# A decoder layer in four token chunks instead of three, with 311 instead of 226 expert pairs placed beside them

## The reference

```python
h = rms_norm(x); q, k, v, u, g_att, g_s5 = split(h @ w_in)
att = diff_attention(q, k, v)              # 8 heads, causal; sampled tokens also read 1024 cached rows
s5y = s5_scan(u)                           # diagonal state space model along the tokens
z = gelu(s5y); s5o = z * sigmoid(z @ w_glu + b_glu)
x = x + (sigmoid(g_att) * (att @ w_proj_att) + sigmoid(g_s5) * (s5o @ w_proj_s5)) @ w_out
h = rms_norm(x)
# PEER: per token 8 heads, each picks 16 of 16384 experts
s1, s2 = (h @ w_query) . sub_keys          # two score rows of 128 per head
eidx, gate = top 16 of the sums of the two top-16 lists, softmax
act = gelu(einsum('thkd,td->thk', expert_u[eidx], h))
x = x + einsum('thk,thkd->td', gate * act, expert_v[eidx])
y = rms_norm(x)
```

## Time and profile before

| | |
|---|---|
| median of the runs | 5216.02 us (2 runs, 5215.28 to 5216.76) |
| the profiled execution | 5215.25 us, its span 5213.5 us, 1.8 us around it |
| VectorE busy | 3092.5 us (59%) |
| TensorE busy | 3691.3 us (71%), mean granted clock 0.852 |
| DMA | 1417.77 MB, 272 GB/s over the span |
| first chunk, second, third, tail | 439, 881, 1562, 1582 us |

### The profile page before, as it was taken

How to read it: one execution, slowest core, us unless ns; L and a number is a source line. 1 busy time by engine, 2 the same in 40 slices (tenths; PEclk the granted TensorE clock), 3 DMA queues, 4 the chain that set the end, 5 groups by cost and what they waited for, 6 DMA issues and landing times. The chain is left out here.

```text
span 5213.5 us, 44142 instructions
## 1 busy us (share of the span) xinstructions
PE 3691.3 (71%) x13504; PEld 2091.9 (40%) x13504; DVE 3092.5 (59%) x6901; ACT 1517.0 (29%) x3777; POOL 1331.2 (26%) x1167
## 2 busy tenths in 40 slices
PE   6964888787766757876755454758777777777776
PEld 4542566564343434434444444424222222222221
DVE  4144211316678756768886555658666666666664
ACT  3111011303244321424432222322333333333333
POOL 0000000002312222322222222224444444444443
PEclk9955569898878878988877777879999999999999
DMA  2013123357855768885578788769999999999997
GB/s 78 34 19 1 3 77 130 108 176 301 347 201 206 303 258 344 330 318 199 201 265 305 304 304 311 285 240 363 420 419 417 415 415 410 414 414 406 408 406 324
DMA packets 282269, 1417.77 MB, mean 272 GB/s; under 512 B 44194, under 2 KB 86658, under 8 KB 144546
## 3 DMA queue, kind: packets, MB, share of 16 engines
q0 software_dynamic: 159344, 1129.94, 54.7%
q1 hardware_dynamic: 122306, 284.90, 16.4%
q10 hardware_dynamic: 384, 0.13, 0.0%
HBM read 1371.57 MB, written 40.93 MB: 271 GB/s over the span
## 5 line engine op out<-in xcount | busy, mean ns | idle before, releaser
L807 POOL DMA_INDIRECT arena<-in_uv,arena x1056 | 1262.8, 1196 | 2652.4 <-DVE arena L918 1730.9
L908 DVE CUSTOM_DVE_ANT_0 arena<-arena 128x1024 f32<-128x1024 f32 x1056 | 1288.5, 1221 | 507.2 <-DMA arena<-in_uv,arena 479.4
L1024 PE MATMUL ps<-arena 128*128 128x512 f32 (+1 forms) x2416 | 1148.5, 621 | 428.9 <-ACT arena L993 428.9
L1091 PE MATMUL ps<-arena 128*128 128x256 f32 (+2 forms) x3456 | 1125.2, 487 | 210.3 <-DMA arena<-in_keys 52.2
L1091 PEld LDWEIGHTS ps<-arena 128*128 128x128 f32 x3456 | 693.8, 204 | 606.5 <-issue 384.8
L1024 PEld LDWEIGHTS ps<-arena 128*128 128x128 f32 (+1 forms) x2416 | 439.0, 191 | 1137.8 <-ACT arena L993 664.1
L918 DVE SCALAR_TENSOR_TENSOR arena<-arena 128x1024 f32<-128x1024 f32 x452 | 577.9, 1279 | 157.7 <-ACT arena L983 157.7
L974 ACT ACTIVATE arena<-arena 128x2 f32<-128x2 f32 x528 | 107.0, 203 | 1689.5 <-DVE arena L908 1689.0
L1683 PE MATMUL ps<-ident,arena 128*128 128x128 f32 x512 | 91.1, 339 | 269.3 <-DMA arena<-in_cache_k 243.8
L983 ACT ACTIVATE arena<-arena 128x1 f32<-128x1 f32 x1056 | 253.3, 287 | 17.9 <-ACT arena L974 0.7
L813 POOL DMA_DIRECT2D arena<-in_iota x1 | 0.7, 715 | 936.7 <-POOLq L1962 936.7
(11 more groups left out here) (249 smaller groups left out, 3762.0 us busy)
## 6 DMA issues: line engine op xcount, KB each, us to landing
arena<-in_w_stat SPq DMA_DIRECT2D x216, 512.0 KB, 6.6
arena<-in_cache_k SPq DMA_DIRECT2D x64, 512.0 KB, 6.6
arena<-in_cache_v SPq DMA_DIRECT2D x64, 512.0 KB, 10.9
arena<-in_w_mov SPq DMA_DIRECT2D x14, 2048.0 KB, 12.7
arena<-in_uv,arena POOLq DMA_INDIRECT x1056, 13.0
arena<-in_x SPq DMA_DIRECT2D x16, 512.0 KB, 4.7
arena<-scr_s POOLq DMA_DIRECT2D x64, 128.0 KB, 12.9
scr_s<-arena SPq DMA_DIRECT2D x16, 384.0 KB, 12.0
```

The costliest lines, as they stand in the source:

```text
L807: pool.indirect_dma_start(ring[s % RING], None, dr["uv"], bass.IndirectOffsetOnAxis(ap=idx[:, g % 4, j:j + 1], axis=0)).then_inc(row_in[s ...
L908: nc.vector.tensor_tensor_reduce(ring[s % RING][:, 0:D], ring[s % RING][:, 0:D], h2r[:, b % 2, :], 1.0, 0.0, ALU.mult, ALU.add, act_in[:, ...
L1024: last = nc.tensor.matmul(ps[0:m, 4 * (b % 2) + c, :], diag[:, n % 4, 0:m], ring[s % RING][:, D + 512 * c:D + 512 * (c + 1)], start=start, ...
L1091: last = nc.tensor.matmul(ps[:, bank, 0:w], wbuf[m % NWB][:, kc * P:(kc + 1) * P], moving[:, kc, :], start=(kc == 0), stop=(kc == KC - 1))
```

## The change

The chunks become four: blocks 0 and 1, 2 and 3, 4 and 5, 6 to 8, which are 256, 256, 256 and 288 columns. Each of the later three has a row of its own in the plan: 82, 88 and 141 pairs, 311 in all, so that 217 stay for the tail. With `PAIRS_FRONT` at 311, the v half of 85 more pairs is added by VectorE instead of TensorE. The three rules for when GpSimd loads score rows, h rows and x rows are rewritten for four chunks.

```diff
-        CHUNKS = ((0, 2), (2, 5), (5, NB))
+        CHUNKS = ((0, 2), (2, 4), (4, 6), (6, NB))
         STAGES = ("glu", "s5", "v", "att", "dec", "ga", "out", "query")
         PAIR_PLAN = ((0, 0, 0, 0, 0, 0, 0, 0),
-                     (6, 12, 7, 24, 0, 12, 5, 16),
-                     (7, 14, 9, 27, 50, 14, 6, 17))
+                     (6, 12, 8, 22, 0, 12, 6, 16),
+                     (7, 13, 8, 24, 0, 13, 6, 17),
+                     (7, 14, 9, 24, 50, 14, 6, 17))
         PAIRS_BEFORE = [0, 0]
         for plan in PAIR_PLAN[1:]:
             PAIRS_BEFORE.append(PAIRS_BEFORE[-1] + sum(plan))
-        PAIRS_FRONT = PAIRS_BEFORE.pop()
+        PAIRS_FRONT = PAIRS_BEFORE[-1]
+        ROWS_AT = [PAIRS_BEFORE[c] + sum(PAIR_PLAN[c][:-1]) for c in range(len(CHUNKS))]
...
         def step_scores(g):
-            return -1 if g < 3 else max(HALF * (g - 3), PAIRS_BEFORE[chunk_of(head_block(g))])
+            return -1 if g < 3 else max(HALF * (g - 3), PAIRS_BEFORE[chunk_of(head_block(g)) + 1])
 
         def step_h2(b):
-            return -1 if b < 2 else max(first_pair(b - 1) + 2, PAIRS_BEFORE[chunk_of(b)])
+            return -1 if b < 2 else max(first_pair(b - 1) + 2, ROWS_AT[chunk_of(b)])
 
         def step_x1(b):
-            return -1 if b < 2 else max(first_pair(b - 1) + 12, PAIRS_BEFORE[chunk_of(b)])
...
+            return -1 if b < 2 else max(first_pair(b - 1) + 12, ROWS_AT[chunk_of(b)])
```

More of the change, by code:

```diff
@@ L754, in step_scores @@
         def step_scores(g):
-            return -1 if g < 3 else max(HALF * (g - 3), PAIRS_BEFORE[chunk_of(head_block(g))])
+            return -1 if g < 3 else max(HALF * (g - 3), PAIRS_BEFORE[chunk_of(head_block(g)) + 1])
         def step_h2(b):
-            return -1 if b < 2 else max(first_pair(b - 1) + 2, PAIRS_BEFORE[chunk_of(b)])
+            return -1 if b < 2 else max(first_pair(b - 1) + 2, ROWS_AT[chunk_of(b)])
         def step_x1(b):
-            return -1 if b < 2 else max(first_pair(b - 1) + 12, PAIRS_BEFORE[chunk_of(b)])
-        for c, (lo, hi) in enumerate(CHUNKS[1:], 1):
-            assert PAIRS_BEFORE[c + 1 if c + 1 < len(CHUNKS) else c] >= 0
-            assert PAIRS_BEFORE[c] <= HALF * (PH * lo - 2), (c, PAIRS_BEFORE)
+            return -1 if b < 2 else max(first_pair(b - 1) + 12, ROWS_AT[chunk_of(b)])
+        for g in range(2, HEADS):
+            assert step_scores(g) <= HALF * (g - 2), (g, step_scores(g))
         def score_sem(g):
```

## The result

The changed kernel takes 5385.78 us (2 runs, 5385.73 to 5385.83), the kernel before 5216.02. The ratio is 1.033, with an interval of 1.031 to 1.036: slower, as forecast, 53 us under the forecast of 5439 and inside its range.

What follows compares the result with a forecast made beforehand. Gathers bound the tail, 5.17 us a pair; pairs with weights hold most chunk stages. From 5215 us, -439 in the tail, +665 in the later chunks and -2 in the first chunk gave 5439 us; 8-in-10 range 5310 to 5540.

Steps and rivals of the forecast that it cites:

- The tail: Stretch after the chunks, bound by gathers: 85 pairs leave it at 5.17 us each, -439 us.
- The stages that transfers hold: Later chunks' `glu`, `s5`, `v`, `ga`, `query`: pairs and weights set their length; +61, +101, +64, +100, +130 us.
- the 4 us taken off for the narrower start: Transfer-bound stages keep the length their pair number gives, less 4 us where the tiles at their start are narrower.
- `out`: Stage of the later chunks: six pairs on two blocks taken at 73 us, three stages 227 us, +58.
- `dec`: Sampled tokens' stage in the last chunk: the same 50 pairs and pages, 589 us, change 0.
- `att`: Attention stages of the later chunks: 70 pairs at 6.07 us of VectorE time, 845 us against 693.7, +151.
- The sentence that failed: A pair costs 5.17 us in the tail; chunks must hide it in idle time, scarcest where work is added.
- Rival 1: Later chunks: lowered clock takes the narrower tiles' gain back and `att` pairs cost more; 5523 to 5594 us, chance 0.18.
- The Trainium skill's warning: TensorE in the chunks: thin tiles between DMA waits let it fall back to its slow clock again and again.
- Rival 2: Later chunks fill to the tail's rate, 415 GB/s, growing +495 us: 5271, up to 5320 us, within 2%; chance 0.14.
- Rival 3: Later chunks: columns set the stages, pairs ride free, only seven stage starts add 105 us: 4881 us, faster; chance 0.07.
- The limit of about 358 GB/s: DRAM limit for one core: by it a tail pair would be 5.86 us and the tail give back 498.

## Why the prediction was right, and where it was not

**The tail.** Forecast -439, measured -440, at 400 GB/s and DMA 0.98. In 1000 us of its middle 385 dot products ran, and VectorE again waited 302 us for gathers, as in the earlier trace rows:

```profile
L909 DVE CUSTOM_DVE_ANT_0 arena<-arena 128x1024 f32<-128x1024 f32 x385 | 471.0, 1225 | 310.8 <-DMA arena<-in_uv,arena 301.6 <-issue 4.1 <-DVE arena L874 1.4
```

**The stages that transfers hold.** Forecast +61, +101, +64, +100, +130 for `glu`, `s5`, `v`, `ga` and `query`, measured +50, +92, +58, +82, +121. The mechanism is the one named: with 12 pairs the stage stands on a floor of 93.6 us that no width changes. The term that was mis-sized most is the 4 us taken off for the narrower start (7 in the second chunk's `query`). Before's wide `s5` stood 14.6 us above the floor and the narrow one 6.1, so the tiles' width was worth 8.5 us; `ga` gained 11.0 and `query` 9.3 in the second chunk. The three kinds with most tiles, `s5`, `ga` and `query`, came out 37 us below the forecast, `glu` 11, and `v`, which has no weight tiles, 6. Over these five kinds the forecast was 53 us too high, which is its whole error; `out` (10 more than forecast) and `dec` (9 less) cancel.

**`att`.** Forecast 845, measured 845.2, with 261, 283 and 301 where its own sum gives 251, 287 and 307. VectorE's share in it was 0.74 in the second chunk and 0.79 in the last. Its composition was not seen: 63 us of the +151 come with the fourth chunk even without pairs.

**`dec`.** Forecast 0, measured -9. That this stage takes further pairs at 1.2 us (38 to 50) to 3.0 us (50 to 66) was not seen either. From 38 to 50 pairs it was the cheapest place of all; from 66 to 80 a pair took 4.5 us.

**The sentence that failed** is the one behind the rows: that the stretches that receive more work have the least idle time, with 85 pairs weighed against the tail's 5.17 us as if they were the whole cost. By themselves they gained 105 us (3.95 us a pair). What cost was the fourth chunk, 276 us, of which 105.5 appear without any pair. The forecast was right in sum since it costed whole stages from rows with both parts in them, and such a sum needs no division. For the same reason it could not show that three chunks with more pairs would be faster than both.

**The other 170 us of the chunk's price** appear only beside pairs. By kind, the four chunks with 226 pairs take more than the three: `query` 67 us, `s5` 53, `ga` 53, `att` 49, `out` 41, `v` 20, `glu` 17, and `dec` 24 less. Without pairs the same differences are 16, 5, 5, 63, 9, 4, 8 and 1 us. So `s5`, `ga` and `query` make up 147 of the 170 us, though they carry only 8 pairs more than before, and `att` nothing. The weight tiles have a part: halving them took 53 us from the change and 24 from the kernel before; doubled and with the slabs (8.4 MB beside 37.7) the added set would be some 70 us (an estimate, from a run with 311 pairs and one with 226). Some 35 us are the 12 pairs that stood outside `dec` in that run. The rest, about 65 us, fits what the floor says, that narrow tiles give back 8.5 us of the 25.7 that they give back without pairs. But tiles and floor are not two separate causes, and no run took the 170 us apart further; how much the low rate at a stage's start adds outside the one `s5` read above is open.

**The rivals.** Rival 1: the clock did fall, from a mean of 0.82 to 0.77 in the chunks with pairs, and `s5` of 256 columns took 69.0 us of matmul time at 0.81 where it takes 56.0 at 1.00. While the matmuls of that `s5` ran, the granted clock fell from full to half speed four times, in before's `s5` once. It cost little there: leaving out half of the tiles' matmuls, 343 us of TensorE time, changed the chunks by 95 us, 61 of them in `att`. No run changed the clock by itself, so what it costs in `att` is open. The Trainium skill's warning (TensorE: Matmul & The Clock Gate, HAM oscillation) thus describes what TensorE did here, but the time of the stages beside pairs hardly followed it. Rival 2's floor of 93 us for `s5` with 12 pairs is the 93.6 of the runs with half the matmuls; the kernel itself stayed 6 us above. Rival 3 needed `s5` under 88 us, below the floor. The limit of about 358 GB/s for one core in the Trainium skill (DMA: Bandwidth & Descriptors, Specifications) doesn't hold in these runs either: 400 GB/s over the tail, 397 over that `s5` with half the matmuls.

**The checks named.** `s5` took 99.7 us (said: 104 to 107; under 95 would have refuted) with TensorE busy 69% of it (said: under 65%). The second chunk took 792 us (797), the three later ones without `dec` 2475.5 (2519), the three `att` 845 (845; under 780 would have refuted). The mean granted clock is 0.811 (below 0.852). The rate over the later chunks is 305 GB/s (297 forecast; over 310 would have refuted), 301 to 311 in the single chunks.

## What to carry to other kernels

Where one change moves work and also cuts the loop beside it finer, price the two apart: a finer loop repeats its fixed loads, and once a stage stands on a floor of transfers, narrower compute gives almost nothing back. The price of work placed beside a loop is not one number: here it ran from 1.2 to some 7 us for the same pair, and climbed as a stage filled. The busy shares of a row alone didn't give it: in the changed kernel `out`, with VectorE at 0.56 and DMA at 0.58 to 0.64, took 5.3 us for a further pair, `dec`, with 0.58 and 0.81, only 1.2. So measure the price by moving a few pairs in one stage, and stop where it reaches the price at the end (5.17 us).

## What was not expected of the hardware

- With half the matmuls, two stages with the same 12 pairs and weights and different matmul widths took the same 93.6 us, at 397 and 391 GB/s, a mixture of 8 KB gathers and 512 KB weight tiles; that is 1 to 3% below the pure gathers of the tail (400 to 404).
- The granted clock, a mean of stretches at full and at half speed, fell with TensorE's busy share over the chunks with pairs: 0.82 at 67% busy before, 0.77 at 57% in the change, 0.71 at 47% with half the matmuls, where the chunks still took 95 us less.
